# Attention: the order of ScalarE's and VectorE's queues, one chunk deeper against the value products

## The reference

```python
s = (jnp.einsum('bgjqd,bgkd->bgjqk', qb, kb) * scale
     - slopes[None, :, :, None, None] * dist.astype(f32))
s = jnp.where(valid, s, -jnp.inf)
return jnp.einsum('bgjqk,bgkd->bgjqd', jax.nn.softmax(s, axis=-1), vb)
```

## Time and profile before

| | before |
|---|---|
| median of 3 runs | 3550.38 us (3548.31 to 3553.31) |
| the profiled execution | 3556.11 us, its span 3554.4 us |
| TensorE busy, products (PE) | 3167.2 us, 89% |
| VectorE (DVE) busy | 1572.4 us, 44% |
| ScalarE (ACT) busy | 1202.8 us, 34% |
| mean granted TensorE clock | 0.946 |

### The profile page before, as it was taken

The page is one execution under the profiler, slowest core; times in us unless marked ns, Lnnn a source line. Parts: engine busy times, 40 slices in busy tenths (PEclk is TensorE's granted clock), DMA queues, the critical chain, the costliest instruction groups (busy, mean ns, idle before and its releaser), DMA issues. The chain is left out here.

```text
span 3554.4 us, 43615 instructions
## 1 busy us (share of the span) xinstructions
PE 3167.2 (89%) x15498; PEld 2608.5 (73%) x15498; DVE 1572.4 (44%) x3479; ACT 1202.8 (34%) x2541; POOL 53.7 (2%) x103
## 2 busy tenths in 40 slices
PE   8998476888899999999999656888898899999999
PEld 6887476666688888887788455766776788888887
DVE  3132766555323232323542166888885323232323
ACT  5232332543222121212442154666664222121211
POOL 0000000000000000000000120000000000000000
PEclk9999787998999999999999677999999999999999
DMA  4334101232112122212363602201201112121212
GB/s 142 107 107 114 34 9 43 64 64 77 46 47 85 48 71 60 83 36 65 90 178 81 122 4 64 65 23 43 54 11 54 36 49 91 45 71 60 75 51 95
DMA packets 266165, 236.81 MB, mean 67 GB/s; under 512 B 44297, under 2 KB 206089, under 8 KB 265961
## 3 DMA queue, kind: packets, MB, share of 16 engines
q1 hardware_dynamic: 265960, 234.18, 23.8%
HBM read 188.80 MB, written 45.15 MB: 66 GB/s over the span
## 5 line engine op out<-in xcount | busy, mean ns | idle before, releaser
L442 PE MATMUL ffn_acc<-m_hi,ffn_w_hi 128*128 128x512 f32 x1408 | 438.6, 392 | 18.7 <-DVE ffn_w_lo L523 18.7
L442 PE MATMUL ffn_acc<-m_lo,ffn_w_hi 128*128 128x512 f32 x1408 | 439.5, 393 | 0.0
L523 DVE TENSOR_TENSOR ffn_w_lo<-ffn_raw,ffn_w_hi 128x1024 fp32r<-128x1024 f32 x88 | 107.8, 1225 | 748.0 <-ACT ffn_w_hi L482 748.0
L442 PE MATMUL ffn_acc<-m_hi,ffn_w_lo 128*128 128x512 f32 x1408 | 438.0, 392 | 0.0
L482 ACT ACTIVATE ffn_w_hi<-ffn_raw 128x1024 fp32r<-128x1024 f32 x88 | 93.4, 1061 | 760.3 <-PE ffn_acc L442 747.3
L1120 PE MATMUL in_acc<-in_w_hi,in_hT_hi 128*128 128x512 f32 (+1 forms) x832 | 330.2, 397 | 1.0 <-DVE in_w_lo L1251 1.0
L1122 PE MATMUL in_acc<-in_w_hi,in_hT_lo 128*128 128x512 f32 (+1 forms) x832 | 324.3, 390 | 0.0
L1121 PE MATMUL in_acc<-in_w_lo,in_hT_hi 128*128 128x512 f32 (+1 forms) x832 | 323.7, 389 | 0.0
L442 PEld LDWEIGHTS ffn_acc<-m_hi,ffn_w_hi 128*128 128x128 f32 x1408 | 265.4, 189 | 78.0 <-DVE ffn_w_lo L523 19.3
L1752 ACT ACTIVATE at_pr<-at_ps_s 128x512 f32<-128x512 f32 x480 | 224.4, 467 | 277.5 <-PE at_ps_s L1682 274.4
L442 PEld LDWEIGHTS ffn_acc<-m_hi,ffn_w_lo 128*128 128x128 f32 x1408 | 265.2, 188 | 59.7
(11 more groups left out here) (296 smaller groups left out, 5287.0 us busy)
## 6 DMA issues: line engine op xcount, KB each, us to landing
ffn_d_raw<-in_ffn_w_down SPq DMA_DIRECT2D x176, 256.0 KB, 2.7
ffn_raw<-in_ffn_w_gate SPq DMA_DIRECT2D x44, 512.0 KB
ffn_raw<-in_ffn_w_up SPq DMA_DIRECT2D x44, 512.0 KB
in_raw<-in_hy_w_in SPq DMA_DIRECT2D x56, 256.0 KB
proj<-in_nat SPq DMA_DIRECT2D x40, 256.0 KB
in_raw<-in_nsa_w_in SPq DMA_DIRECT2D x40, 256.0 KB
at_qa<-at_turned SPq DMA_DIRECT2D x320, 0.5 KB
at_qa<-q1T_hi SPq DMA_DIRECT2D x16, 264.0 KB
```

The source lines that it names most:

```text
L442: ins = nc.tensor.matmul(acc[:, m, half, :].rearrange("p (t c) -> p t c", c=P), w[:, m, k, :], h[:, half * S:(half + 1) * S, k, :], start= ...
```

## The change

In the loops of ScalarE and VectorE inside `attention_stage` the offsets grow by one: exponentials are issued four chunks ahead of the value products' step in place of three, high copies and low parts two ahead in place of one. What runs ahead of the loops takes one exponential, one high copy and one low part more. TensorE's and SyncE's order, all buffers and all waits stay as they are.

```diff
--- before.py
+++ after.py
@@ -1774,17 +1774,18 @@
                 act.wait_ge(bias_tr, n + 1)
                 nc.scalar.activation(branches[n].cols[0][:], bias_tr_of[n], ACT.Copy).then_inc(cols_hi if dilated else cols_done, 1)
             split(0, 0)
-            for c in range(3):
+            for c in range(4):
                 exps(0, c)
             high(0, 0)
+            high(0, 1)
 
             def body(it, first, last):
                 for c in range(C):
                     for i, s in events(split_events, it, c, last):
                         split(i, s)
-                    for i, n in ahead(it, c + 3, last):
+                    for i, n in ahead(it, c + 4, last):
                         exps(i, n)
-                    for i, n in ahead(it, c + 1, last):
+                    for i, n in ahead(it, c + 2, last):
                         high(i, n)
                     for i, u in ended(it, c - 1, first):
                         evacuate(i, u)
@@ -1891,12 +1892,13 @@
                     maximum(0, m)
             split(0, 0)
             low(0, 0)
+            low(0, 1)
 
             def body(it, first, last):
                 for c in range(C):
                     for i, s in events(split_events, it, c, last):
                         split(i, s)
-                    for i, n in ahead(it, c + 1, last):
+                    for i, n in ahead(it, c + 2, last):
                         low(i, n)
                     for i, m in events(maxima_at, it, c, last):
                         maximum(i, m)
```

## The result

The change made the kernel slower: 3638.2 us in the median (3635.3 to 3645.1), against 3551.9 for the kernel before in the same group; the ratio is 1.0244 (95% interval 1.0230 to 1.0257). The direction was forecast; the size, +86 us, is twice the forecast +41. The profiled span grew from 3554.4 to 3643.0 us.

What follows compares the result with a forecast made beforehand. TensorE, busy 83% and 86% of the two attention stages, was taken as the bound, with waits making its idle time. Dilated waits 44.5, clock 5 and second stage -8.5 gave +41 us: 3591 us, range 3563 to 3618.

Steps and rivals of the forecast that it cites:

- The round within one step: Dilated stage: the third maximum of a step waits for a full round TensorE, ScalarE, VectorE inside the same step.
- Term 2: Dilated stage, step 3 of a head's steps 0 to 11: first maximum 1.82 us later, once a head.
- Term 3: Dilated stage, step 6 of a head's steps 0 to 11: third maximum 1.84 us later, once a head.
- Term 1: Dilated stage, step 8: the row of maxima that comes back by DMA is 1.76 us later, once a head.
- Term 4: Dilated stage, step 7 of a head's steps 0 to 11: third maximum 0.93 us later, once a head.
- term "-8.5": Second attention stage: 8.5 us gained over 16 causal pairs (0.11 each) and 16 window pairs (0.42 each).
- I take three, 5 us: Dilated stage: three more stretches at the lower clock behind the longer waits, costing 5 us in all.
- rival B: Dilated stage: half of TensorE's work goes at 1.2 GHz, 30 us in place of 5; 3616 us; chance 0.13.
- A: The main forecast: dilated waits, small clock loss, second-stage gain; 3591 us, own range 3574 to 3606; chance 0.68.
- C: Faster: second stage's low-part waits vanish without output delay (-33), dilated round overlaps present waits (+15); 3532 us; chance 0.08.
- D: Both stages: depth not used, ScalarE waits for TensorE anyway, pace kept within 5 us; 3550 us; chance 0.05.
- E: Only the dilated stage's first and third terms are real: 25 us, less 9; 3566 us; chance 0.06.

## Why the prediction was right in direction and wrong in size

**The reading of the queues held.** The round within one step is in the trace where it was forecast. TensorE after the change, one dilated head in order of time:

```profile
728.80 0.40 PE L1682 MATMUL at_ps_s<-dil_cols_lo,at_ident_r 128*128 128x512 f32 x1
...
731.34 0.44 PE L1662 MATMUL at_ps_m<-at_ka,at_qa 96*128 96x384 f32 x1 [1.66 <-DVE at_top L1842]
...
737.24 0.28 PE L1682 MATMUL at_ps_s<-dil_cols_lo,at_ident_r 128*128 128x256 f32 x1
739.85 0.69 PE L1662 MATMUL at_ps_m<-at_ka,at_qa 96*128 96x512 f32 x1 [2.33 <-DVE at_top L1842]
...
744.92 0.69 PE L1662 MATMUL at_ps_m<-at_ka,at_qa 96*128 96x384 f32 x1 [1.71 <-DVE at_top L1842]
...
748.40 0.63 PE L1682 MATMUL at_ps_s<-dil_cols_lo,at_ident_r 128*128 128x512 f32 x1
...
755.74 0.50 PE L1682 MATMUL at_ps_s<-at_qb,at_kb 128*128 128x512 f32 x1 [2.34 <-DMA at_qa<-at_turned]
```

- Term 2, step 3: from the scores' end (729.20) to the maximum 2.14 us; forecast 2.13.
- Term 3, step 6: 737.52 to 739.85, 2.33; forecast 5.69 - 3.37 = 2.32.
- Term 1, rows: scores' end 749.03 to the row's arrival 6.71, before 5.09: +1.62; forecast +1.76.
- Term 4, step 7: 5.07 here, at the lower clock; 4.01 where the throwaway products hold it; forecast 3.95.
- The sum a head: 6.35 forecast. With the throwaway products heads take 30.8 in the mean for 24.6 before, +6.2, and for 23.8 in the kernel before with products, +7.0. Over the stage that is +43.4 or +48.0 against 44.5. That term of the sum was right.
- The waits themselves, as forecast under "What would show it", were not all there: those for the row grew by 0.8 each and not by 1.7 (17.4 for 11.3 in all), and those for the query reload fell from 10.2 to 0.9, while the same products took 32 us more of busy time.

**Second stage, the wait that moves.** Forecast was a causal pair of 17.23 us with nearly nothing left of the removed 1.1; it takes 17.38 (2375.98 to 2393.36). The window pair was put at 15.25 and takes 15.51 (2465.12 to 2480.63). So the term "-8.5" should have been about -2 by these two pairs; with the throwaway products the stage is +3.8, 12 us above the term and within my bound of +10. VectorE after the change, at the end of a causal pair, shows the mechanism as forecast: the low part of chunk 16 waits for ScalarE's copy and the output, which before started at once, stands behind it.

```profile
2406.71 0.69 DVE L1858 TENSOR_TENSOR at_p_lo<-at_pr,at_p_hi 128x512 fp32r<-128x512 f32 x1 [0.66 <-ACT at_p_hi L1759]
2407.32 0.18 DVE L1870 RECIPROCAL at_rl<-at_ps_t 128x4 f32<-128x4 f32 x1
```

**The step that failed: the clock.** "I take three, 5 us" stands where the runs show 12.5 to 17.1 us in the dilated stage; and in the second stage, where I had no term for it at all, 23.5 to 24.1. By the larger figures that is 41 in place of 5, or 36 of the some 47 us by which the span grew beyond the sum (88.6 for 41); the rest is the second stage's waits, 12 above their term, less 1 in the dilated stage. The granted clock shows how much there was to price: 91 us of the dilated stage went at the lower level (16 before), in every head but the last, and 75 us of the second (10 before). I had seen that in a causal pair two waits of about 1 us (1.11 at the third maximum, 0.92 at the values) become a single one, and counted only that their sum stays. It does not stay without consequence. TensorE after the change, a causal pair's third maximum and two value products behind it:

```profile
2410.69 0.49 PE L1662 MATMUL at_ps_m<-at_ka,at_qa 96*128 96x512 f32 x1 [2.06 <-DVE at_top L1845]
...
2413.40 0.63 PE L1697 MATMUL at_ps_o<-at_p_hi,at_v_hi 128*65 128x512 f32 x1
2413.83 0.63 PE L1697 MATMUL at_ps_o<-at_p_hi,at_v_lo 128*65 128x512 f32 x1
```

The windows of 4 us around them (columns as above, the granted clock third from the end):

```profile
2408.00:2412.00 4.00, 1.94 (x11) 1.16 (x9) 3.48 (x9) 2.35 (x5) 0.00 (x0) 1.00 0.01 2
2412.00:2416.00 4.00, 3.96 (x16) 2.93 (x16) 2.74 (x8) 0.90 (x2) 0.00 (x0) 0.57 0.01 4
2416.00:2420.00 4.00, 4.00 (x14) 2.77 (x14) 2.96 (x10) 1.50 (x4) 0.00 (x0) 0.58 0.01 2
2420.00:2424.00 4.00, 4.00 (x30) 3.55 (x29) 2.81 (x10) 2.72 (x8) 0.00 (x0) 1.00 0.00 0
```

TensorE waits 2.06 us; the granted clock then goes to the 1.2 GHz level for most of two windows, products of 512 columns stand 0.43 us apart (0.23 at full clock), and the pair's evacuations are 20.10 us apart (2404.26 to 2424.36) where the two pairs ahead of it have 17.3 and 17.4. Five pairs of the second stage are like this one (19.7 to 20.1 us), and the turns between rounds take 1 to 2 us more. Before, the third maximum's wait was 1.1 us, and no pair outside the turns took more than 17.6 us. The Trainium skill ("TensorE: Matmul & The Clock Gate", section on HAM oscillation) has the mechanism, waits between bursts that throttle the array again, and I had it as rival B. The trace agrees in kind in the dilated stage, where the clock falls in every head with such waits; in the second stage it falls behind some of them and not behind each, and once in a window pair without a wait above 1.1 us (17.5 us for 15.4, clock 0.80). So what the products show is that the clock is the loss and that filling the waits gives it back; which waits bring it down is not shown. I gave B 0.13, confined it to the dilated stage, and argued against it with waits of 0.7 to 1.5 us at full clock, which says nothing of waits of 2.3.

**The rivals.** A's waits were right in the dilated stage, 12 us too low in the second, and its time wrong by the clock. B's mechanism came, in both stages: less than its 30 us in the dilated one, and some 24 in the second, where it had nothing. C fell: the low parts' wait did vanish, the output's delay came with it. D and E fell. The range ended at 3618, B's time with the clock priced in one stage only. (The chances of A, B and E add to 0.87, where the prediction says 0.86.)

**A version that beats both.** Copies and low parts two ahead with exponentials left at three: 3535.8 and 3540.7 us in two groups, 0.4 to 0.55% under the kernel before and 2.7 to 2.8% under the change.

## What to carry to other kernels

In a set of in-order queues, ask of a deeper lookahead which item of the other engine now stands ahead of the latency-bound one: here it was the exponential, not the copy, and one number of the three gave all of the loss. Follow the ring with start and end times from the trace; that gave these waits to 0.2 us. Then look at the granted clock and at how TensorE's waits are distributed, and not only at their sum: with two waits of about 1 us joined to one of 2.1, the pairs in which the clock fell cost 3 us more. The longest wait alone is no rule: the kernel with scores six ahead has shorter ones and the lowest clock.

## What the hardware showed that I had not expected

Five products whose result nobody reads, put into each long wait, made the kernel 39 us faster (3638.2 to 3598.8) with the ring behind the waits as long as before. Four of them in the long waits of the kernel before, whose regular waits are 1.1 to 1.5 us, gave nothing (3553.1 beside 3554.4). And a high copy that directly follows its own exponential on ScalarE cost 10% more of ScalarE's busy time in the second stage (391.7 for 355.6 us) than one with another exponential between.
